# Two mixers of one kernel: a masked product in two halves, two constant products taken out, level masks of half the columns

## The reference, cut to what matters

```python
kk = jnp.einsum('bhnid,bhnjd->bhnij', kb, k) * decay
sol = lax.linalg.triangular_solve(kk, rhs, left_side=True, lower=True, unit_diagonal=True)
...
seg = jnp.exp(jnp.where(lower, cum[:, :, :, None] - cum[:, :, None, :], -jnp.inf))
cb = jnp.einsum('bnigs,bnjgs->bnijg', Cc, Bc)
y_diag = jnp.einsum('bnijg,bnijgr,bnjgrp->bnigrp', cb, seg, dtc[..., None] * xc)
```

## Time and profile before

| what | value |
|---|---|
| runs of the kernel before | 2760.86, 2763.43, 2766.92 us (median 2763.43) |
| the profiled execution: its own time / its span | 2760.54 us / 2758.5 us |
| busy in the span: PE, DVE, ACT, POOL | 95%, 46%, 19%, 21% |
| the mixers' stage, from its first to its last instruction | about 343 to 596 us |
| busy in those 253 us: PE, DVE, ACT, POOL | 224.96, 113.91, 63.16, 140.59 us |
| granted TensorE clock: mean of the execution / of the stage | 0.989 / 0.99 of full speed |
| HBM traffic in the stage | 2 GB/s |

### The profile page before, as it was taken

The page is one execution under the profiler, slowest core; times in us unless marked ns, Lnnn a source line. Parts: engine busy times, 40 slices in busy tenths (PEclk is TensorE's granted clock), DMA queues, the critical chain, the costliest instruction groups (busy, mean ns, idle before and its releaser), DMA issues. The chain is left out here.

```text
span 2758.5 us, 46734 instructions
## 1 busy us (share of the span) xinstructions
PE 2614.7 (95%) x20654; PEld 1988.3 (72%) x20654; DVE 1272.5 (46%) x1976; ACT 520.2 (19%) x1032; POOL 585.4 (21%) x328
## 2 busy tenths in 40 slices
PE   6999888989999999999888899999999999999998
PEld 4555577754888887444777658888878764888886
DVE  2213234443899944223677554442241373544333
ACT  3222122221111101113455210000010172100001
POOL 0000066520000000001222114344424200433342
PEclk9999999999999999999999999999999999999999
DMA  7223100021212123120000012222222201222120
GB/s 295 86 102 149 62 2 2 2 93 61 89 69 87 67 82 126 46 86 37 34 3 3 2 61 92 92 77 77 92 83 87 92 1 40 83 92 91 66 88 31
DMA packets 17368, 195.32 MB, mean 71 GB/s; under 512 B 1896, under 2 KB 3048, under 8 KB 5392
## 3 DMA queue, kind: packets, MB, share of 16 engines
q1 hardware_dynamic: 17168, 192.34, 18.6%
HBM read 190.22 MB, written 2.12 MB: 70 GB/s over the span
## 5 line engine op out<-in xcount | busy, mean ns | idle before, releaser
L3237 PE MATMUL psum<-arena,weight_ring 128*128 128x256 f32 x3072 | 671.0, 379 | 2.4 <-ACT arena L3127 2.4
L3237 PEld LDWEIGHTS psum<-arena,weight_ring 128*128 128x128 f32 x3072 | 582.8, 190 | 85.1 <-ACT arena L3127 4.7
L1832 PE MATMUL psum<-arena,weight_ring 128*128 128x256 f32 x1584 | 348.2, 381 | 5.0 <-DVE arena L2008 4.0
L1832 PEld LDWEIGHTS psum<-arena,weight_ring 128*128 128x128 f32 x1584 | 301.6, 191 | 48.7 <-issue 6.4
L2361 POOL TENSOR_TENSOR arena<-arena,consts_sb 128x512 f32<-128x512 f32 x48 | 64.8, 1357 | 882.0 <-ACT arena L2710 691.2
L492 PE MATMUL psum<-arena,weight_ring 128*128 128x512 f32 (+1 forms) x672 | 247.9, 528 | 2.9 <-DMA weight_ring<-in_w_in 2.7
L492 PEld LDWEIGHTS psum<-arena,weight_ring 128*128 128x128 f32 x672 | 127.3, 192 | 115.6 <-issue 101.7
L3336 POOL TENSOR_TENSOR weight_ring<-arena,weight_ring 128x1024 f32<-128x1024 f32 x32 | 79.3, 2477 | 379.3 <-PE psum L3237 379.3
L3326 POOL TENSOR_TENSOR arena<-weight_ring 128x1024 f32<-128x1024 f32 x32 | 76.9, 2404 | 290.5 <-POOLq L3020 261.2
L229 PE MATMUL psum<-arena,weight_ring 128*128 128x512 f32 x320 | 137.8, 592 | 0.0
L3359 ACT ACTIVATE arena<-psum 128x512 f32<-128x512 f32 (+1 forms) x24 | 12.6, 524 | 621.0 <-PE psum L3237 621.0
(11 more groups left out here) (478 smaller groups left out, 3785.8 us busy)
## 6 DMA issues: line engine op xcount, KB each, us to landing
weight_ring<-in_mlp_up SPq DMA_DIRECT2D x16, 2048.0 KB, 7.9
weight_ring<-in_mlp_down SPq DMA_DIRECT2D x16, 2048.0 KB, 7.9
weight_ring<-in_ada SPq DMA_DIRECT2D x12, 2048.0 KB, 12.1
weight_ring<-in_gate_up SPq DMA_DIRECT2D x11, 2048.0 KB, 8.2
weight_ring<-in_w_in SPq DMA_DIRECT2D x7, 2048.0 KB, 11.8
weight_ring<-in_w_o SPq DMA_DIRECT2D x4, 2048.0 KB, 7.8
weight_ring<-in_w_kv SPq DMA_DIRECT2D x4, 2048.0 KB, 7.9
weight_ring<-in_down_a SPq DMA_DIRECT2D x4, 1536.0 KB, 6.5
```

The lines of the kernel that those rows point to most:

```text
L1832: mm = pe.matmul(g.banks[i][:, pair * half:(pair + 1) * half], left[:, j, pair * P:(pair + 1) * P], right(j), start=first and j == 0, stop ...
L3237: mm = pe.matmul(g.banks[i][:, pair * HALF:(pair + 1) * HALF], left[:, j, pair * P:(pair + 1) * P], right(j), start=first and j == 0, stop ...
```

## The change

Three edits, all in `stage_mixers`.

1. The masked product. DVE's one multiplication of `mts` (128x1024) in a `ydiag` use becomes two of 128x512. The first works on heads 0 to 3 and stands in DVE's order at the slot of `seg` j = 1, one use earlier; it waits for the exponential of `seg` j = 0. The second works on heads 4 to 7 and stands where the one stood. PE waits for both (`m4` counts 4 for each tile in place of 2).
2. The two constant products (128x512) ahead of L1229 are taken out at all 8 `ydiag` uses. Those of 128x256 in `idle_bank` stay.
3. The level masks. At level 0, and at level 1 of tile 0, POOL still multiplies all 512 columns. At every other level (29 of 36 masks) it does one multiplication for each direction, each over only the half of the columns that `level_products` uses: 128 columns, in runs of 2, 4, 8, 16 or 32. Columns that are not written keep what an earlier mask left in them. The counts of `ltm` become 11 for each tile, less one (`masked`).

```diff
+    def used_columns(blocks, d, lvl):
+        return blocks[:, 4 * d:4 * d + 4, :].rearrange("p b (x t m) -> p b x t m", t=2, m=1 << lvl)[:, :, :, 1 - d, :]
+
+    def masked(i, lvl):
+        return 11 * i + 2 * lvl + 1 - ((i, lvl) >= (0, 1))
...
                     mask = g.c.lvl[:, lvl * P:(lvl + 1) * P].rearrange("p (d n) -> p d n", d=2)
-                    pool.tensor_tensor(grid(ltm[lvl % 2]), grid(lt[i % 2]), lanes(mask), ALU.mult).then_inc(s.ltm, 1)
+                    if lvl == 0 or (i, lvl) == (0, 1):
+                        pool.tensor_tensor(grid(ltm[lvl % 2]), grid(lt[i % 2]), lanes(mask), ALU.mult).then_inc(s.ltm, 1)
+                        return
+                    for d in (0, 1):
+                        high = half_blocks(mask[:, d, :], lvl, 1 - d)
+                        pool.tensor_tensor(used_columns(ltm[lvl % 2], d, lvl), used_columns(lt[i % 2], d, lvl),
+                                           bcast(high, 1, [P, 4, 64 // (2 << lvl), 1 << lvl]), ALU.mult).then_inc(s.ltm, 1)
...
                 def level_x(i, lvl):
-                    pe.wait_ge(s.ltm, 6 * i + lvl + 1)
+                    pe.wait_ge(s.ltm, masked(i, lvl))
...
                     elif kind == "ydiag":
-                        for _ in range(2):
-                            keep_busy(pe, g, bank, SEQ)
-                        pe.wait_ge(s.m4, 2 * m + d + 1)
+                        pe.wait_ge(s.m4, 4 * m + 2 * d + 2)
...
                     if i >= 2:
-                        dve.wait_ge(s.ltm, 6 * (i - 1))
+                        dve.wait_ge(s.ltm, masked(i - 2, 5))
...
+                    if (kind == "seg" and j == 1) or kind == "ydiag":
+                        half = 0 if kind == "seg" else 1
+                        dve.wait_ge(s.taken, n)
+                        m4 = mts[:, 4 * half:4 * half + 4, :]
+                        dve.tensor_tensor(m4, m4, bcast(cbm[:, d, half, :], 1, [P, 4, P]), ALU.mult).then_inc(s.m4, 1)
                     if kind == "seg":
                         return
-                    if kind == "ydiag":
-                        dve.wait_ge(s.taken, n)
-                        m4 = mts.rearrange("p (a h) n -> p a h n", a=2)
-                        dve.tensor_tensor(m4, m4, bcast(cbm[:, d, :, :], 2, [P, 2, 4, P]), ALU.mult).then_inc(s.m4, 1)
```

More of the change, by code:

```diff
@@ L1002, in mask_level @@
                     mask = g.c.lvl[:, lvl * P:(lvl + 1) * P].rearrange("p (d n) -> p d n", d=2)
-                    pool.tensor_tensor(grid(ltm[lvl % 2]), grid(lt[i % 2]), lanes(mask), ALU.mult).then_inc(s.ltm, 1)
+                    if lvl == 0 or (i, lvl) == (0, 1):
[5 more added lines that the diff above has]
+                                           bcast(high, 1, [P, 4, 64 // (2 << lvl), 1 << lvl]), ALU.mult).then_inc(s.ltm, 1)
                 def tt_init(i):
-                    pool.wait_ge(s.ltm, 6 * i + 1)
+                    pool.wait_ge(s.ltm, masked(i, 0))
                     if i >= 2:
```

## The result

The changed kernel took 2768.24 us (median of 20 runs, 2762.59 to 2778.20) against 2763.54 for the kernel before (20 runs). I had forecast 2757.1, 6.3 us faster, with a range of 2750 to 2766. The sign is wrong and the time lies outside the range.

The account below looks back on a forecast made before the run. The prediction took the stage to be a chain carried by PE. Earlier output products 8.1 us plus masks 1.4 less clock falls 3.2 made 6.3 us less, 2757.1 us, range 2750 to 2766.

Parts of the forecast that it names:

- The stage is a chain that PE carries: Mixers' stage: PE's order is fixed, so a microsecond PE gets back at one place moves everything behind it.
- 9.5 for the whole change: Whole change if the clock holds: 8.1 us from earlier output products plus 1.4 us from masks.
- The gains at the eight places: Output product L1229 at the eight ydiag uses starts earlier, by 0.4 to 1.7 us each, 8.1 us in sum.
- Place 1: First ydiag use: the second half ends shortly behind POOL's long product; gain 0.3 to 0.6 us, taken 0.4.
- The masks: POOL's split level masks: a pair takes 0.93 us for 1.28, saving 0.35 at four PE waits, 1.4 us.
- The clock: PE idle at the ydiag uses without constant products: two more falls to half clock, about 1.6 us each, 3.2 us lost.
- six falls: Upper bound on clock falls in the stage: one for each PE idle stretch of 0.6 us or more.
- Slower: Sign of the whole change: slower was given 0.05, as half of the rival that the masks turn late.
- the masks were not late: Rival on POOL's level masks: short runs cost like whole masks, a pair 2.55 us, total 2766.1 us; chance 0.10.
- POOL holds DVE up: Rival on DVE's masked-product halves: they finish only behind long POOL instructions, total gain 2.0 us, 2761.4 us; chance 0.20.

Follow-up runs that it names:

- e8: e5 with three more constant products in iteration 6, ahead of the level products of level 2, 3 and 5: 2758.45 us, ratio 0.9976.
- e3: The kernel before with only the masked product in two halves; constant products and whole masks stay: 2764.14 us, ratio 0.9998.
- e4: The kernel before with only the split level masks of the used half columns: 2764.83 us, ratio 1.0004.
- e5: The changed kernel with the two constant products put back at the forward outputs only (places 1, 3, 5, 7): 2757.46 us, ratio 0.9977.
- e7: The changed kernel with one constant product of 512 columns put in at every place: 2761.02 us, ratio 0.9987.

## Why the prediction was wrong

**The stage is a chain that PE carries: right.** The earlier starts did reach the stage's end. In e8, with no half clock in the stage, it is 240.8 us; the stage before, less the 1.7 us that its half clock cost, is 249.3. That is 8.5 us, where I had summed 9.5 for the whole change and e8 keeps some constant products.

**The gains at the eight places: right in size.** Each measured from the same instruction ahead in both traces (the second exponential at places 1, 2 and 4, the last matmul group ahead on PE at the rest), the gains are 0.44, 0.87, 0.31, 1.38, 0.47, 1.17, 0.71 and 1.74 us for places 1 to 8, 7.1 in sum against 8.1. Places 3, 5 and 7 are the short ones. At 3 and 5 the second half took 0.88 and 0.86 us, not 0.65, and at place 7 POOL held up L1397 ahead of it. Place 1 went as worked out: POOL's product held the second half until 360.19, and it ended at 360.74.

```profile
358.25 1.94 POOL L1031 TENSOR_TENSOR weight_ring<-consts_sb,arena 128x1024 f32<-128x1024 f32 x1 [1.51 <-PE psum L1233]
358.83 1.91 DVE L1465 TENSOR_TENSOR weight_ring<-weight_ring 128x512 f32<-128x512 f32 x1 [0.39 <-ACT weight_ring L1356]
```

**The masks: right.** A pair was taken at 0.93 us and measures 0.87 to 0.98 alone, 1.0 on average; PE's waits fell by 2.0 us where 1.4 was taken. The estimate that I had made from the figures of the Trainium skill (GPSIMD Engine Reference, Elementwise — side-by-side cycle accounting) gave 0.68. The measurement lies by the rows of the trace: a short POOL product costs more than those figures for a long one give. That e3 and e4 would each show no gain alone was not foreseen.

**The clock: the step that failed.** I took "two more falls than before, 3.2 us", at "about 1.6 us" a fall. The number of falls was nearly right: four stretches in place of one. Their length was not. I priced each by the only one that the stage of before had, 3.40 us. They lasted 6.8, 13.6, 10.2 and 6.8 us, and the price is up to 17.7 us less the 1.7 of before: up to 16 us where I had 3.2. The bound "six falls", 9.6 us, was built on the same unit, so the range was too narrow at its upper end.

The profile of before could have warned me. Outside the stage it has longer stretches at half clock: one of 10.2 us that begins 11 us behind the stage, and one of 6.8 us in which PE was busy throughout. The windows of the kernel before at these two:

```profile
606.75:610.17 3.42, 1.89 (x8) 1.78 (x8) 2.36 (x4) 0.59 (x3) 0.00 (x0) 0.50 1.04 441
610.17:613.58 3.41, 2.48 (x4) 1.17 (x4) 3.18 (x5) 0.00 (x0) 0.00 (x0) 0.50 0.78 332
613.58:616.99 3.41, 3.41 (x5) 1.33 (x4) 0.74 (x2) 0.00 (x0) 0.00 (x0) 0.50 0.00 0
1224.57:1227.98 3.41, 3.41 (x10) 2.23 (x10) 2.75 (x5) 0.00 (x0) 0.00 (x0) 0.50 0.00 0
1227.98:1231.39 3.41, 3.41 (x5) 1.35 (x4) 0.00 (x0) 0.00 (x0) 0.00 (x0) 0.50 0.00 0
```

The length of a fall was taken for a constant from one sample of one stage, while the same trace showed two and three times that length. That the falls of the changed kernel would be of the long kind could not be read from it.

**The sum with the right term.** Over the runs the mean clock fell from 0.989 to 0.984. At two levels that is twice 0.005 of 2768 us, 28 us more at half clock, which costs up to 14. Less the forecast gain of 9.5 this leaves 4.5 us slower; the medians give 4.7. That they lie so close is in part luck: a step of 0.001 in the clock is 2.8 us in this sum, and in the two profiled executions 11 of the 45 us more at half clock lie outside the stage. The stage itself closes better. Its 249.3 us at full clock, less the 9.1 that the eight places (7.1) and the masks (2.0) measure, make 240.2; e8 has 240.8, and e5, less 3.4 for its half clock, 240.3. The changed kernel's 255.8 are 15.6 above 240.2. So the four stretches cost 15.6 of the 17.7 us that they can, 13.9 more than the 1.7 of before, where I had taken 3.2. The control runs say the same without arithmetic: edit 2 alone costs 16.7 us, and putting its products back into the changed kernel gives 7.2.

**The rivals.** Slower did come, but not by the one that I had put there: the masks were not late. "POOL holds DVE up" describes e3 and e4, and in part the changed kernel, where it lengthened eight of sixteen halves; but there it took at most 1.0 us of the 8.1 and is not the loss. The rule of the Trainium skill behind it (GPSIMD Engine Reference, Key points: POOL's SBUF interfaces are shared with VectorE) agrees with the pairs shown above, 1.53 us for 0.65 in e3, 2.80 for 1.22 in e4 and 2.44 for 0.96 at place 7.

## What to carry to other kernels

- A constant product in front of a wait can be worth far more than the time that it blocks. Here its removal made the products start as early as worked out, and a clock that stayed down for 7 to 14 us at a time took more than that back. Take such filler out only where the wait is gone (the backward places, once the halves were there), and leave it where PE still waits 2 us.
- Do not price a fall of the clock by one sample. Read the granted clock over the whole profile, not only over the stage that changes, and take the longest stretch at half for the bad case: here 10.2 us stood in the trace of before, and 13.6 came.
- A shorter instruction on POOL moves the next long one. Look which product of VectorE with two SBUF inputs it then meets: in e4 it met one more at place 5 and one less at place 7.

## What the runs showed of the hardware that I had not expected

The granted clock stayed at half (1.2 GHz) while PE was busy nearly throughout: 12.88 of 13.6 us in the changed kernel, 19.05 of 20.5 in e7. In the same stage of the kernel before it was back after 3.4 us, in e5 after 3.4 us twice. Small products alone do not explain it: the kernel before was at half for 6.8 us from 1224.6 on too, with PE busy throughout and about 15 records, most of them 128x512, where the changed kernel's last stretch has 92. What decides this I did not settle. And idle time alone did not decide whether it fell: 2.24 us at place 1 of the changed kernel did not slow the products behind it, 1.24 us in e7 did.
